# The low part of the retention state moves from GpSimd to VectorE

## What is computed

```
def step(state, qkv):
    qi, ki, vi = qkv
    scores = jnp.einsum('bhnd,bhmd->bhnm', qi, ki) * decay_in
    o = (jnp.einsum('bhnm,bhmv->bhnv', scores, vi)
         + jnp.einsum('bhnd,bhdv->bhnv', qi, state) * decay_q[:, :, None])
    state = (state * decay_chunk[:, None, None]
             + jnp.einsum('bhmd,bhmv->bhdv', ki * decay_k[:, :, None], vi))
    return state, o
```

## Time and profile before

| | before |
|---|---|
| median of 3 runs (lowest, highest) | 2122.24 us (2121.58, 2123.37) |
| span of the profiled execution | 2121.2 us |
| TensorE busy | 2070.5 us, 98% of the span |
| VectorE busy | 1237.7 us, 58% |
| ScalarE busy | 846.1 us, 40% |
| GpSimd busy | 233.8 us, 11% |
| mean granted TensorE clock | 0.996 of full |
| chain of work that ended last: TensorE, VectorE | 92%, 4% |

### The profile page before, as it was taken

The page is one execution under the profiler, slowest core; times in us unless marked ns, Lnnn a source line. Parts: engine busy times, 40 slices in busy tenths (PEclk is TensorE's granted clock), DMA queues, the critical chain, the costliest instruction groups (busy, mean ns, idle before and its releaser), DMA issues.

```text
span 2121.2 us, 27026 instructions
## 1 busy us (share of the span) xinstructions
PE 2070.5 (98%) x10400; PEld 1760.7 (83%) x10400; DVE 1237.7 (58%) x1453; ACT 846.1 (40%) x1051; POOL 233.8 (11%) x172
## 2 busy tenths in 40 slices
PE   7999999999999999999799999999999999999998
PEld 6888999988888888887688887897788888888887
DVE  6422444467655444312977777847887887853433
ACT  6122555511135543411444443345544445442322
POOL 0000000000000000011445544300000000000000
PEclk9999999999999999999999999999999999999999
DMA  4323333323223223535333334731222221274443
GB/s 164 120 84 125 150 145 131 119 102 116 79 99 119 103 95 118 178 119 196 87 115 107 96 114 129 257 130 60 90 89 79 79 99 61 102 263 149 145 140 122
DMA packets 167553, 258.61 MB, mean 122 GB/s; under 512 B 8256, under 2 KB 119232, under 8 KB 167488
## 3 DMA queue, kind: packets, MB, share of 16 engines
q1 hardware_dynamic: 150352, 191.67, 27.0%
q0 software_dynamic: 17136, 66.06, 7.9%
HBM read 187.45 MB, written 70.25 MB: 121 GB/s over the span
## 4 chain that ended last, share of the span: by engine, by line
PE 92%; DVE 4%; issue 1%; ACT 1%; DMA 1%; SPq 0%; DVEq 0%; ACTq 0%
PE ps L261 30%; PE ps L263 30%; PE ps L262 30%; PE ps L943 1%; DMA raw<-w_ret_o 0%; DVE mxf L2067 0%; DVE mix L2073 0%; PE ps L322 0%; PE ps L974 0%; PE ps L896 0%; DMA raw<-w_in 0%; ACT ws L240 0%; DVE scs L2024 0%; DVE ws L244 0%; DVE gt L2222 0%
## 5 line engine op out<-in xcount | busy, mean ns | idle before, releaser
L244 DVE TENSOR_TENSOR ws<-raw,ws 128x2048 fp32r<-128x2048 f32 x46 | 105.4, 2291 | 249.5 <-ACT ws L240 247.5
L261 PE MATMUL ps<-xs,wx 128*128 128x512 f32 x612 | 239.6, 392 | 5.5 <-ACT ub L1495 3.2
L262 PE MATMUL ps<-xs,wx 128*128 128x512 f32 x612 | 238.8, 390 | 0.0
L263 PE MATMUL ps<-xs,wx 128*128 128x512 f32 x612 | 238.7, 390 | 0.0
L261 PE MATMUL ps<-actv,ws 128*128 128x512 f32 x576 | 224.6, 390 | 0.3 <-DVE actv L350 0.3
L262 PE MATMUL ps<-actv,ws 128*128 128x512 f32 x576 | 224.1, 389 | 0.0
L263 PE MATMUL ps<-actv,ws 128*128 128x512 f32 x576 | 224.1, 389 | 0.0
L240 ACT ACTIVATE ws<-raw 128x2048 fp32r<-128x2048 f32 x46 | 87.9, 1912 | 214.8 <-PE ps L263 133.5
L1246 ACT ACTIVATE wx<-raw 128x1024 fp32r<-128x1024 f32 (+1 forms) x110 | 98.9, 901 | 177.9 <-PE ps L263 93.7
L263 PE MATMUL ps<-ws,actv 128*128 128x256 f32 x512 | 144.9, 283 | 0.0
L262 PE MATMUL ps<-ws,actv 128*128 128x256 f32 x512 | 144.9, 283 | 0.0
(11 more groups left out here) (260 smaller groups left out, 4815.9 us busy)
## 6 DMA issues: line engine op xcount, KB each, us to landing
raw<-w_in SPq DMA_DIRECT2D x80, 512.0 KB, 4.5
scr<-ost POOLq DMA_DIRECT2D x32, 1024.0 KB, 4.7
raw<-w_up SPq DMA_DIRECT2D x44, 512.0 KB, 3.9
raw<-w_down SPq DMA_DIRECT2D x44, 512.0 KB, 4.4
scr_h<-vt POOLq DMA_DIRECT2D x11, 1024.0 KB, 4.3
hraw<-scr_h SPq DMA_DIRECT2D x22, 512.0 KB, 5.4
scr_v<-ost POOLq DMA_DIRECT2D x8, 1024.0 KB, 4.6
qkv<-scr SPq DMA_DIRECT2D x64, 128.0 KB, 2.9
```

What stands on the lines that cost most here:

```text
L244: dve.tensor_tensor(ws[:, slot, LO, 0:n], raw[:, slot, 0:n], ws[:, slot, HI, 0:n].bitcast(F32), ALU.subtract).then_inc(w_split[slot], 1)
L261: pe.matmul(out, w(HI), x(HI), start=first, stop=False, skip_group_check=True)
L262: pe.matmul(out, w(HI), x(LO), start=False, stop=False, skip_group_check=True)
L263: return pe.matmul(out, w(LO), x(HI), start=False, stop=last, skip_group_check=True)
```

## The change

state_lo leaves GpSimd's instruction list and enters VectorE's. On VectorE it stands after the state update and its first projection part, and after the split_lo of steps 3 and 5 where there is one, and ahead of the second projection part. The operands, the type and the two semaphores (it waits for s_hi and raises s_sp) are the same. It is done in steps 0 to 6 of each head, 28 times in all. Nothing else is changed, and no DMA is moved.

```diff
-            def state_lo(h, j):
-                slot = j % 2
-                pool.wait_ge(sem["s_hi"], h * 7 + (j + 1))
-                pool.tensor_tensor(sts[:, slot, LO, :, :], stt[:, :, :], sts[:, slot, HI, :, :].bitcast(F32),
-                                   ALU.subtract).then_inc(sem["s_sp"], 1)
-
             for j in range(NCH):
                 lo_parts(0, j)
                 if j == 1:
                     store_rnno(3)
-                if j:
-                    state_lo(0, j - 1)
             with pool.Fori(1, HEADS) as h:
                 for j in range(NCH):
                     lo_parts(h, j)
-                    if j:
-                        state_lo(h, j - 1)
...
+            def state_lo(h, j):
+                slot = j % 2
+                dve.wait_ge(sem["s_hi"], h * 7 + (j + 1))
+                dve.tensor_tensor(sts[:, slot, LO, :, :], stt[:, :, :], sts[:, slot, HI, :, :].bitcast(F32),
+                                  ALU.subtract).then_inc(sem["s_sp"], 1)
+
...
                 if (j == 3 and not first) or j == 5:
                     split_lo(dve, h + PAIR_RETO, 0 if j == 3 else 1)
+                if j < 7:
+                    state_lo(h, j)
                 for n in parts[1:]:
                     accumulate(*n)
```

## The result

The changed kernel takes 2127.87 us (median of 13 runs, 2125.51 to 2130.16) against 2122.47 us for the kernel before (13 runs): a ratio of 1.0026, 95% interval 1.0019 to 1.0034. It is slower by 5.4 us; 2127.4 us was forecast, 5.2 more than before. The profiled execution took 2126.8 us, 5.6 more than the one before. TensorE's mean granted clock is 0.996 as before.

A forecast was written before the change was run, and what follows sets the result against it. TensorE, busy for 98% of the span, was taken as the bound. The terms 3.42 + 1.26 + (1.14 + 0.3) - 0.9 gave +5.2 us, so 2127.4 us (+0.25%), range 2124.8 to 2129.6.

The forecast's parts named there:

- Step 4: Heads 1 to 3: step 3's state_lo lengthens VectorE's row before ktm, TensorE's hole grows 0.56 to 1.7 us; +3.42 us.
- Step 6: Heads 1 to 3: step 5's state_lo makes TensorE's update 0.31 us late, 0.42 with a longer first matmul; +1.26 us.
- The other steps of the loop: Heads 1 to 3, steps without split_lo: the delay is gone before anything reaches TensorE; cost 0.
- Head 0, end: Existing hole before step 6 takes the full 1.14 us; step 5's gate_lo hi copy comes 0.3 late.
- Head 0, up to step 4: L2024's stall exchanged for equal work; step 1 race and clock open: -0.9 us, between -2.2 and +1.
- the race: Head 0, step 1: L1980 against GpSimd's L705; won, head 0 gives 1.4 us back; lost, 0.15.
- rival c: Holes of 1.7 us in steps 4 and 6 halve the clock, four times some 2 us: +13, 2135 us; chance 0.06.
- signs of being wrong: A turn of 80.4 us, state_lo above 1.3, clock under 1 after 1050 us, or head 0 shorter by over 2.
- Rival (b): Relief wins: L2024's stalls go (8.5 us), ScalarE's copy hides state_lo; -2.4, 2119.8 us; chance 0.03 faster, 0.03 within 0.2%.
- Rival (d): No change in time because VectorE has idle time in every step: 0, 2122 us; chance 0.02.
- Rival (a): Head 0 gives -2.2 (race won, clock full), step 5 costs under 0.42; sum +2.5 to +4.2 us; chance 0.28.

The follow-up runs named there:

- experiments 3: Changed kernel, but only the 7 subtractions in steps with a weight split on VectorE, the other 21 on GpSimd: 2128.07 us, ratio 1.0029 to the kernel before.
- 8: Changed kernel with the subtraction of step 3 in heads 1 to 3 done twice, one after the other: 2132.89 us, ratio 1.0049 to the kernel before.
- 2: Changed kernel, but GpSimd keeps the subtraction in the 7 of 28 steps with a weight split: 2121.17 us, ratio 0.9994 to the kernel before.
- 5: Changed kernel, all 28 on VectorE, the 7 of weight-split steps one step later, behind the scores' low part: 2121.20 us, ratio 0.9993 to the kernel before.
- the second: Profile from running the unmodified changed kernel again: profiled run 2124.0 us; median 2126.78 us, ratio 1.0026 to the kernel before.
- experiment 7: Kernel before, with GpSimd writing zeros (memset) in place of its subtraction, leaving out the state's low part: 2114.68 us, ratio 0.9968 to the kernel before.

## Why the prediction was right

**Step 4** (3.42 us expected): right. The hole grew by 1.12 us in each turn, from 1.14 us of VectorE's row with nothing to hide it; experiments 3 and 8 price it, and 2 and 5 take it away.

**Step 6** (1.26): right in kind and size. TensorE came 0.30 us late, and from step 4 to step 1 of the next head 49.46 us passed for 49.02. Together the two terms were to give 4.68; from 1083.37 to the last hole of the stage the first profile shows 4.4 and the second 4.7. The difference is mostly in that last hole, ahead of the last head's transposes (1.35 us in the first profile, 1.59 in the second, 1.52 before).

**The other steps of the loop** (0): right. Experiment 2 has 21 of the 28 on VectorE and a turn of 80.4 us.

**Head 0, end** (1.14 + 0.3): right. From the state update of step 5 to TensorE's update in step 6 it takes 8.05 us for 6.93, and from the state update of step 4 to that of step 5 9.31 for 9.04. The second is the 0.3: gate_lo in step 5 now waits for ScalarE's hi copy, as predicted.

```profile
1041.03 0.69 DVE L1986 TENSOR_TENSOR yh<-ych,yh 128x512 fp32r<-128x512 f32 x1 [0.17 <-ACT yh L1372]
```

**Head 0, up to step 4** (-0.9): right in kind, mis-sized. The state updates (L2043 in the kernel before) stood at 1011.51, 1021.04, 1029.69, 1038.67 and 1047.71 in steps 1 to 5, and stand now (L2039) at 1009.49, 1018.16, 1027.07, 1035.74 and 1045.05. The first came 1.4 earlier (the start of the stage taken off: the race, won), the second another 0.9 (from 1010 to 1020 us, step 2, the clock was 0.97 where it had been 0.66), and steps 3 and 4 moved by 0.3 either way. That is -2.3 where I took -0.9, of an interval that began at -2.2. The corner came true that I had priced at both ends and then not chosen.

**The clock** (rival c, 0.06): a slow stretch behind a hole exists here, against my ground for putting it aside, and one of the prediction's own signs of being wrong, a granted clock under 1 after 1050 us, came in the first profile. One hole of 1.66 us without a slow stretch behind it says nothing of one of 1.89. It cost 1.6 us in the first profile and none in the second, where rival (c) had 2 us four times. In these runs no hole of 1.69 us or less in steps 4 of the loop was followed by slow matmuls; of three of 1.9 (head 0, in the two profiles of the change and in that of experiment 8) two were, one of 2.16 was not, and of three of 2.94 two were. What decides between those is open: the length of the hole alone does not. In head 0 too the slow stretches lie at other places in the two profiles of the same code (1019.7 and 1037.5 us in the first, 1001.5 and 1028.7 in the second).

So the forecast of 5.2 us met the 5.4 measured partly by luck. From the first update of head 0 to the last hole of the stage the first profile is 5.1 us longer than the kernel before, with head 0 up to its hole at -0.9 where the terms gave +0.5, and 1.6 of clock that stood in no term; the second, without that slow stretch, is 4.2 us longer. What the clock costs on average over the runs was not measured.

**Rival (b)**, relief wins, was ruled out on the right ground: the relief is real (8.2 us, experiment 7), but in head 0 the update ends before ScalarE's copy starts, so waiting and work take its place. **Rival (d)** fell with the holes. **Rival (a)**'s corner in head 0 came true, but not its sum: in the first profile the clock took it back, and the medians lie 5.4 us apart.

## What to carry to other kernels

What an instruction costs on an engine with idle time depends on what stands right behind it, place by place: 21 of 28 here cost nothing that could be measured, 7 cost all of it (5.9 us by themselves), and a place one step later made them free too. Before choosing a place, read in every variant of the step what the next waiter on another engine hangs on (in step 4 ktm, in step 1 gate_lo), and put the instruction where its own input is already there, behind work that would fill the wait. Relief from contention is worth only what is left when the moved work has taken its own place on the chain.

## What the runs showed of the hardware

A VectorE instruction of one element per partition with two SBUF inputs (L1980, L1970 after the change) takes 0.16 us alone and up to 1.19 when a GpSimd subtraction is running; one started 0.11 us ahead of the subtraction and was not held. GpSimd's memset of 128 x 1024 takes 0.95 us, and a VectorE subtraction that ran inside it was not held; GpSimd's two-input subtraction of the same size takes 2.4 us. After holes of 1.9 to 2.9 us in an otherwise dense stream of matmuls the granted clock was sometimes 0.56 to 0.70 over the next 3.3 to 3.9 us, at 1.6 us of cost each, and sometimes 1.00, for the same code.
